# Weight parts of the first and last expert in another order, and the last sums of a transformer layer shared with GpSimd

## What is computed

```python
h2 = rms_norm(x, norm2_g) * (1.0 + sc2) + sh2
# router: each token gets 2 of 16 experts, with weights g_w * top_w
hid = silu(h2 @ w_gate[e]) * (h2 @ w_up[e])        # 1024 -> 512
out = hid @ w_down[e]                               # 512 -> 1024
x = x + gt2 * (weight1 * out1 + weight2 * out2)     # a token's two experts
y = rms_norm(x, final_g)
```

## Time and profile before

| | |
|---|---|
| time, median of 3 runs (lowest, highest) | 816.15 us (814.02, 816.53) |
| the profiled execution: its time, its span | 814.35 us, 812.5 us |
| busy in the span: TensorE, VectorE, ScalarE, GpSimd | 88%, 65%, 50%, 16% |
| mean granted TensorE clock | 0.937 of full speed |

### The profile page before, as it was taken

How to read it: one execution, slowest core, us unless ns; L and a number is a source line. 1 busy time by engine, 2 the same in 40 slices (tenths; PEclk the granted TensorE clock), 3 DMA queues, 4 the chain that set the end, 5 groups by cost and what they waited for, 6 DMA issues and landing times. The chain is left out here.

```text
span 812.5 us, 10457 instructions
## 1 busy us (share of the span) xinstructions
PE 713.2 (88%) x3772; PEld 543.0 (67%) x3772; DVE 531.0 (65%) x799; ACT 405.4 (50%) x602; POOL 128.2 (16%) x168
## 2 busy tenths in 40 slices
PE   2898999899999989999996578999999999999800
PEld 1237998849998855555543456888888888888600
DVE  5346526369422046574545549999999999999548
ACT  1455533421223144554432337878787787877333
POOL 2000000000022028544220120111211111220000
PEclk9999999999999989999997579999999999999955
DMA  9993115112378383000003997999999999997073
GB/s 321 408 402 143 40 65 207 59 58 104 131 149 270 139 313 154 1 1 27 27 27 109 383 347 276 348 373 375 384 376 392 387 392 378 389 375 272 36 277 129
DMA packets 67196, 183.75 MB, mean 226 GB/s; under 512 B 4592, under 2 KB 4624, under 8 KB 63824
## 3 DMA queue, kind: packets, MB, share of 16 engines
q1 hardware_dynamic: 58080, 161.39, 53.6%
q0 software_dynamic: 7312, 19.61, 6.9%
q10 hardware_dynamic: 1760, 2.17, 0.9%
HBM read 175.26 MB, written 14.19 MB: 233 GB/s over the span
## 5 line engine op out<-in xcount | busy, mean ns | idle before, releaser
L1424 DVE TENSOR_TENSOR WL<-slot,WH 128x1024 fp32r<-128x1024 f32 x192 | 223.4, 1221 | 1.6 <-ACT WH L987 0.8
L987 ACT CAST WH<-slot 128x1024 fp32r<-128x1024 f32 x192 | 187.2, 1056 | 0.0
L1626 PE MATMUL bank<-WH,xgTh 128*128 128x512 f32 x256 | 102.6, 401 | 4.5 <-DVE WL L1424 3.0
L1626 PE MATMUL bank<-WL,xgTh 128*128 128x512 f32 x256 | 101.1, 395 | 0.0
L1626 PE MATMUL bank<-hTh,WP 128*128 128x384 f32 (+1 forms) x320 | 99.1, 310 | 2.2 <-DVE hT L1140 2.2
L1626 PE MATMUL bank<-WH,xgTl 128*128 128x512 f32 x256 | 101.0, 394 | 0.0
L1626 PE MATMUL bank<-hTh,WL 128*128 128x384 f32 (+1 forms) x320 | 98.8, 309 | 0.0
L1626 PE MATMUL bank<-hTl,WP 128*128 128x384 f32 (+1 forms) x320 | 98.8, 309 | 0.0
L1530 PE MATMUL bank<-slot,big 128*128 128x512 f32 (+1 forms) x224 | 92.1, 561 | 1.6 <-issue 1.6
L1539 PE MATMUL bank<-ident,big 128*128 128x128 f32 x424 | 62.2, 287 | 14.0 <-DMA big<-h_scratch,big 8.0
L474 DVE TENSOR_TENSOR WL<-slot,WP 128x1024 fp32r<-128x1024 f32 x24 | 29.3, 1241 | 64.8 <-ACT WP L468 64.3
(11 more groups left out here) (226 smaller groups left out, 1055.4 us busy)
## 6 DMA issues: line engine op xcount, KB each, us to landing
slot<-in_w_gate SPq DMA_DIRECT2D x16, 2048.0 KB, 14.4
slot<-in_w_up SPq DMA_DIRECT2D x16, 2048.0 KB, 16.9
slot<-in_w_down SPq DMA_DIRECT2D x16, 2048.0 KB, 15.6
slot<-in_w_ada SPq DMA_DIRECT2D x12, 2048.0 KB, 13.0
slot<-in_w_in SPq DMA_DIRECT2D x6, 2048.0 KB, 17.6
big<-in_x SPq DMA_DIRECT2D x2, 2560.0 KB, 20.1
big<-y_scratch SPq DMA_DIRECT2D x5, 1024.0 KB, 9.0
big<-m_scratch POOLq DMA_DIRECT2D x8, 512.0 KB, 9.3
```

Source lines behind the costliest of these rows:

```text
L987: act.copy(WH[:, high_half(w, s), r, :], quarter(s, w, r)).then_inc(high_ok[w], 1)
L1424: dve.tensor_tensor(WL[ESLOT[3 * s + w]][:, r, :], quarter(s, w, r), WH[:, high_half(w, s), r, :].bitcast(F32), ALU.subtract).then_inc(low ...
L1626: ins = pe.matmul(out, l[u], r[v], start=first and i == 0, stop=last and i == 2)
```

## The change

Three things are changed.

- **First expert (m == 0).** ScalarE makes the high parts of expert 1's gate behind silu, ahead of the casts of expert 1's rows; VectorE makes all four low parts of it behind the low parts of expert 0's up, ahead of its product silu times up.
- **Last expert (m == NE).** ScalarE makes the high parts of expert 15's down ahead of the cast hidTh, and VectorE the low parts ahead of hidTl.
- **Tail.** The results are loaded in ten halves of 512 KB. ScalarE weights the first result of tiles 0 and 1 as before, and both results of tiles 2 to 4; GpSimd adds the two weighted results of these three tiles, and VectorE goes on with the multiply by gt2 (before L1505). ScalarE weights three tiles ahead of the first root.

```diff
--- before.py
+++ after.py
@@ -58,6 +58,7 @@
 WQ, WK, WV, WX0, WX1, WVH = range(6)
 HY = [WVH, WX1, WX0]
 ADA_GROUPS, ADA_PARTS = 3, 4
+SUMMED = range(2, NT)
 AW = 2048
 QUAD = 32
 
@@ -434,7 +435,8 @@
         sil_ok, hid_ok = sem("silu_ok"), sem("hid_ok")
         hidT_full, hh_ok, hl_ok = sem("hidT_full"), sem("hidT_high_ok"), sem("hidT_low_ok")
         y_out = [sem("y_out0"), sem("y_out1")]
-        yab_in = [sem(f"results_in{t}") for t in range(NT)]
+        yab_in = [[sem(f"results_in{t}{k}") for k in range(2)] for t in range(NT)]
+        f_sum = sem("results_summed")
         f_a, sidx_ok, dest_ok = sem("first_weighted"), sem("scatter_idx_ok"), sem("dest_ok")
         g2row_in, pn_ok = sem("g2row_in"), sem("probs_normed")
         x1_sq = sem("x1_squared")
@@ -604,7 +606,8 @@
             sp.wait_ge(stores_ok, 1)
             table = y_dram.rearrange("(k t p) n -> p t k n", k=2, p=P)
             for t in range(NT):
-                sp.dma_start(yab[:, t], table[:, t]).then_inc(yab_in[t], 16)
+                for k in range(2):
+                    sp.dma_start(yab[:, t, k], table[:, t, k]).then_inc(yab_in[t][k], 16)
             for t in range(NT):
                 sp.wait_ge(f_ok, t + 1)
                 sp.dma_start(outs["y"][t * P:(t + 1) * P, :], x[:, t, :]).then_inc(f_out, 16)
@@ -752,6 +755,9 @@
                 with pool.Fori(1, NT) as p:
                     one_pass(p)
             pool.sem_inc(stores_ok, 1)
+            for t in SUMMED:
+                pool.wait_ge(f_a, SUMMED[0] + 2 * (t - SUMMED[0] + 1))
+                pool.tensor_tensor(yab[:, t, 1], yab[:, t, 1], yab[:, t, 0], ALU.add).then_inc(f_sum, 1)
 
 
         @block.scalar
@@ -1004,14 +1010,17 @@
                     act.wait_ge(used[0], n * 4 + 4)
                     wait_past(act, hid_ok, n)
                     act.activation(sil, bank[2][:, :], ACT.Silu).then_inc(sil_ok, 1)
+                if m == NE:
+                    high_parts(2, n - 1, 1 - s, used[1], (n - 1) * 4)
                 if m != 0:
                     act.wait_ge(hidT_full, n)
                     act.copy(hidTh[:, :, :].rearrange("p a b -> p (a b)"), bank[4][:, :]).then_inc(hh_ok, 1)
-                    if m == NE:
-                        high_parts(2, n - 1, 1 - s, used[1], (n - 1) * 4)
-                    else:
+                    if m != NE:
                         high_parts(2, n - 1, 1 - s, used[0], n * 4)
-                if m is None or m + 1 < NE:
+                if m == 0:
+                    high_parts(0, n + 1, 1 - s, used[1], n * 4)
+                    rows_high(n + 1)
+                elif m is None or m + 1 < NE:
                     rows_high(n + 1)
                     high_parts(0, n + 1, 1 - s, used[1], n * 4)
                 if m != 0:
@@ -1035,15 +1044,23 @@
             with act.If(v > 0):
                 with act.Fori(1, NT) as p:
                     one_pass(p)
-            for t in range(NT + 1):
-                if t < NT:
-                    act.wait_ge(yab_in[t], 16)
-                    act.activation(yab[:, t, 0], yab[:, t, 0], ACT.Copy, scale=wts[:, 0, t:t + 1]).then_inc(f_a, 1)
-                if t > 0:
-                    q = t - 1
-                    act.wait_ge(f_cmb, t)
-                    link(act.activation(sqd, x[:, q, :], ACT.Square, scale=1.0 / 32.0, accum_out=ss[:, 0, q:q + 1]))
-                    act.activation(ss[:, 1, q:q + 1], ss[:, 0, q:q + 1], ACT.Sqrt, bias=epsb[:, :]).then_inc(f_rt, 1)
+            def weighted(t):
+
+                for k in range(2 if t in SUMMED else 1):
+                    act.wait_ge(yab_in[t][k], 16)
+                    act.activation(yab[:, t, k], yab[:, t, k], ACT.Copy, scale=wts[:, k, t:t + 1]).then_inc(f_a, 1)
+
+            def root(t):
+
+                act.wait_ge(f_cmb, t + 1)
+                link(act.activation(sqd, x[:, t, :], ACT.Square, scale=1.0 / 32.0, accum_out=ss[:, 0, t:t + 1]))
+                act.activation(ss[:, 1, t:t + 1], ss[:, 0, t:t + 1], ACT.Sqrt, bias=epsb[:, :]).then_inc(f_rt, 1)
+            for t in range(3):
+                weighted(t)
+            for t in range(NT):
+                root(t)
+                if t + 3 < NT:
+                    weighted(t + 3)
 
 
         @block.vector
@@ -1431,11 +1448,16 @@
                     slots_of(n + 2, i * 2 + (s + 2), s)
                 if m != NE:
                     low_parts(1, n, s)
+                if m == 0:
+                    low_parts(0, n + 1, 1 - s)
+                if m == NE:
+                    low_parts(2, n - 1, 1 - s)
                 if m != 0:
                     dve.wait_ge(hh_ok, n)
                     dve.tensor_tensor(hidTl[:, :, :].rearrange("p a b -> p (a b)"), bank[4][:, :],
                                       hidTh[:, :, :].rearrange("p a b -> p (a b)").bitcast(F32), ALU.subtract)\
                        .then_inc(hl_ok, 1)
+                if m != 0 and m != NE:
                     low_parts(2, n - 1, 1 - s)
                 if m != NE:
                     dve.wait_ge(used[1], n * 4 + 4)
@@ -1445,13 +1467,14 @@
                 following = m is None or m + 1 < NE
                 if following:
                     rows_low(n + 1)
-                    low_parts(0, n + 1, 1 - s, range(2))
+                    if m != 0:
+                        low_parts(0, n + 1, 1 - s, range(2))
                 if m != NE:
                     keep_rows(n, s)
                 if more:
                     dve.wait_ge(sidx_ok, n + 1)
                     numbers(n + 2, s)
-                if following:
+                if following and m != 0:
                     low_parts(0, n + 1, 1 - s, range(2, 4))
                 if m != 0:
                     dve.wait_ge(used[2], n * 4)
@@ -1498,10 +1521,14 @@
             dve.wait_ge(tail_in, 48)
             for t in range(NT + 1):
                 if t < NT:
-                    dve.wait_ge(f_a, t + 1)
                     first, second = yab[:, t, 0], yab[:, t, 1]
-                    link(dve.scalar_tensor_tensor(out=second, in0=second, scalar=wts[:, 1, t:t + 1], in1=first,
-                                                  op0=ALU.mult, op1=ALU.add))
+                    if t in SUMMED:
+                        dve.wait_ge(f_sum, t - SUMMED[0] + 1)
+                    else:
+                        dve.wait_ge(f_a, t + 1)
+                        dve.wait_ge(yab_in[t][1], 16)
+                        link(dve.scalar_tensor_tensor(out=second, in0=second, scalar=wts[:, 1, t:t + 1], in1=first,
+                                                      op0=ALU.mult, op1=ALU.add))
                     link(dve.tensor_tensor(second, second, gt2[:, t // CT, :], ALU.mult))
                     dve.tensor_tensor(x[:, t, :], x[:, t, :], second, ALU.add).then_inc(f_cmb, 1)
                 if t > 0:
```

## The result

The changed kernel takes 820.38 us (median of 5 runs, 819.61 to 821.38); the kernel before took 816.01 us in 5 runs beside them (814.02 to 816.53). The ratio is 1.0062, with a 95% interval of 1.0042 to 1.0082: slower by 0.6%, about 5 us by the ratio and 4.4 by the medians. The forecast was 821.0 us and slower.

A forecast was written before the change was run, and what follows sets the result against it. TensorE, busy 88% of the span, was taken to bound the kernel, and VectorE the tail. 0.2 + 3.6 + 1.1 = 4.9 us on the 816.15 us median gave 821.0 us; the 8-in-10 range was 816.4 to 824.2.

The forecast's parts named there:

- First expert: Expert 0 to 1: last gate quarter and VectorE's product replace the first quarter, so TensorE's wait stays; +0.2 us.
- Last expert: Last down product: quarters stay behind the copy of expert 14's result and delay hidTh and hidTl; +3.6 us.
- Halves: Tail: ten 512 KB loads for five of 1024 let VectorE start at 782.35 instead of 783.58; -1.2 us.
- Sums: Tail: GpSimd's sums stop VectorE, 2.4 us each less what it idles anyway; with halves +1.1 us.
- No hold between the engines: Tail: GpSimd sums beside VectorE without stopping it; tail -3.3 us, sum +0.5, 816.6 us; chance 0.12.
- Down quarters that do run early: Last expert: quarters fill ScalarE's 6.49 idle us before the copy; -1.6 in place of +3.6; chance 0.05.
- The slow clock over the whole product: Last expert: slow clock covers the entire down product after the longer idle; +7.9, 824.0 us; chance 0.08.
- Sum: Whole kernel: first expert 0.2, last expert 3.6 and tail 1.1 make 4.9 us; 821.0 us on the median.

The follow-up runs named there:

- the kernel that only writes: The changed tail, experts as before, with GpSimd writing zeros to unread memory in place of its three sums; ratio 0.9947 against the kernel before.
- the quarters three and one: Kernel before, with quarters 0 to 2 of expert 1's gate behind silu and the fourth behind the rows, on both engines; ratio 0.9963.

## Why the prediction was right, step by step

- **First expert, forecast +0.2.** The profile shows +0.11 (9.59 us from silu to TensorE's start, for 9.48), by the mechanism that was given: quarter, product and rows one behind the other. Right.
- **Last expert, forecast +3.6.** 3.71 (14.49 us between the copies of the last two results, for 10.78). Of it 3.43 are the later start (3.5 forecast) and about 0.3 the clock (0.1 forecast): it was already down when the product began and came back at 773.3, 3.9 us in. The order of the queue, a copy that waits ahead of all that was moved, decided it. The experiment that moves the quarters over that copy shows the other side: -4.1 us from the same instructions (3.2 in the profile, half of it the clock).
- **Halves, forecast -1.2.** VectorE's start is 0.95 earlier, the first half lands 3.7 us after its issue (3.4 forecast), the last 11.1. Slightly oversized. By the runs of the halves alone (-0.2 us, -1.9 to 1.4) the gain isn't shown; it stands on the profiles.
- **Sums, tail +1.1 in all.** 1.46 in the profile of the changed kernel and 1.55 and 1.57 in the two others with this tail; by the runs 1.1 and 0.4, both with intervals that hold zero. The hold exists and lasts 1.9 to 2.15 us of a sum of 2.34, a little less than I took (2.4); VectorE's wait for the first root was 2.15 us for 1.6. From its first instruction to its last VectorE took 28.07 us where the sum had 28.15 (782.35 to 810.5), and that is partly luck: errors cancelled. The holds were shorter, a dropped instruction saves 1.31 us from start to start (787.31 to 788.62 before) and not 1.20, and against that stand the longer wait for the root and a tile of 5.11 us (792.41 to 797.52 before) where the prediction counted 5.03. One row was read a little wrong as well: GpSimd's 0.90 us from 348.45 end 0.3 us behind VectorE's product, not 0.4. The sign of the whole came from the last expert, not from this term.
- **Rivals.** No hold between the engines: fallen, by the stretched instructions and the kernel that only writes; and that kernel shows what would be had without one: 33.12 us for 36.05, 2.9 less where the rival had 3.3. Down quarters that do run early: not in this change, but true of the place. The slow clock over the whole product: it covered 3.9 of 7.64 us.
- **Sum, forecast +4.9.** 5.24 in the profile, 4.4 by the medians; 820.38 us lies 0.6 under the forecast.

## What to carry to other kernels

Before work is moved ahead in a queue, look at what stands in front of it: work that is put behind an instruction that waits starts no earlier, and what it has overtaken starts later. The idle time was ahead of the copy, so the quarters had to go over the copy. And a free engine can cost more than it takes over: in the changed kernel two of GpSimd's three sums held VectorE, which works on two operands from SBUF there, for 1.9 and 2.0 us, where each sum saved it 1.3.

## What the runs showed that I had not expected

- The same idle time of TensorE, 3.0 to 3.1 us, was followed by a slow stretch of about 3.4 us at 16 of its 18 places in the twelve profiles and by none at two: at expert 1 in the first expert's order alone, and at the last expert with the quarters three and one. Each time it was worth about 1.5 us. What decides it is left open; a single profile can't be read to better than this where such a wait lies.
- A shorter wait doesn't keep the clock up for certain either: after the 1.8 us of the kernel with three quarters ahead it fell 1.3 us behind the restart, to half, for 3.4 us (columns as above):

```profile
492.00:495.40 3.40, 3.40 (x10) 2.63 (x9) 3.40 (x6) 2.33 (x3) 1.98 (x1) 0.50 0.93 328
```

- Runs of one kernel differ along with the clock: of 81 runs of the kernel before that stand beside the experiments, the 14 with a mean granted clock of 0.939 have a median of 813.6 us, the 40 with 0.937 815.5, the 6 with 0.933 818.9.
- After 6.45 us of idle the slow stretch was twice as long (766.5 to 773.3), but 2.8 us of it had passed before the product began. The longer idle cost the product 0.3 us, not 3.
- Whether an add or the sum on the other engine starts first turned on 0.04 us, and moved 2 us from one engine to the other.
